# Two transformer blocks on one core: dense ones in TensorE's waits, the root spread by row tiles, weight splits moved into the last expert chunk, and two sums moved

## What is computed

```python
# first block
h = rms_norm(x, norm1_g) * (1 + sc1) + sh1
conv_out = conv_module(...)      # 31 taps, layer_norm, silu, @ w_conv_out
x = x + g1 * (mixed @ w_out)
h2 = rms_norm(x, norm2_g) * (1 + sc2) + sh2
x = x + g2 * moe_ffn(h2, ...)    # top 4 of 32
x = rms_norm(x, final_g)
# second block
x = layer_norm_2(x, ln_emb_g, ln_emb_b)
for layer in range(2):
    mix = hybrid_mixer(x, ...)   # head_group_norm of both retention directions inside
    x = layer_norm_2(ALPHA * x + mix, ln1_g, ln1_b)
    ffn = swiglu(x) if layer == 0 else moe_swiglu(x)     # top 2 of 8
    x = layer_norm_2(ALPHA * x + ffn, ln2_g, ln2_b)
```

## Time and profile before

| | |
|---|---|
| median of 3 runs | 2365.82 us (2364.69 to 2372.74) |
| profiled execution, its own time | 2366.55 us |
| span of the profiled execution | 2364.8 us |
| PE busy (matmul) | 2252.2 us, 95% of the span |
| DVE, ACT, POOL busy | 719.8, 620.7, 395.9 us |
| HBM read | 686.53 MB, mean 291 GB/s |
| mean granted clock of TensorE | 0.975 |

### The profile page before, as it was taken

How to read it: one execution, slowest core, us unless ns; L and a number is a source line. 1 busy time by engine, 2 the same in 40 slices (tenths; PEclk the granted TensorE clock), 3 DMA queues, 4 the chain that set the end, 5 groups by cost and what they waited for, 6 DMA issues and landing times.

```text
span 2364.8 us, 36121 instructions
## 1 busy us (share of the span) xinstructions
PE 2252.2 (95%) x13778; PEld 1384.6 (59%) x13779; DVE 719.8 (30%) x1376; ACT 620.7 (26%) x901; POOL 395.9 (17%) x371
## 2 busy tenths in 40 slices
PE   7999899999999999999998999999999989999898
PEld 5887744444444444444446998899998863333333
DVE  4864322222222222222226244212215341111013
ACT  2142111111111111111115671443368011111111
POOL 2000000000000000000004751688586000000000
PEclk9999799999999999999998999999999989999998
DMA  9972399999999999989994533555454375999752
GB/s 359 380 251 107 90 391 418 418 418 418 418 418 418 418 417 418 418 336 407 418 418 140 161 108 107 168 189 179 126 178 126 138 273 229 390 404 392 278 232 79
DMA packets 223487, 688.71 MB, mean 291 GB/s; under 512 B 28330, under 2 KB 117362, under 8 KB 187570
## 3 DMA queue, kind: packets, MB, share of 16 engines
q1 hardware_dynamic: 221776, 685.82, 75.7%
q10 hardware_dynamic: 1490, 1.61, 0.2%
q0 software_dynamic: 144, 0.20, 0.0%
HBM read 686.53 MB, written 1.05 MB: 291 GB/s over the span
## 4 chain that ended last, share of the span: by engine, by line
PE 66%; DMA 14%; SPq 11%; DVE 6%; issue 2%; ACT 1%; POOL 0%; ACTq 0%; DVEq 0%; POOLq 0%
PE PS L1071 16%; DMA RAW<-in_w_exp_in 10%; PE PS L698 9%; SPq L465 7%; PE PS L687 6%; PE PS L672 6%; PE PS L1173 6%; PE PS L1035 4%; PE PS L1184 3%; SPq L487 3%; DMA W<-in_w_ada 3%; PE PS L1373 3%; PE PS L1054 2%; DMA W<-in_moe_w 2%; PE PS L742 1%
## 5 line engine op out<-in xcount | busy, mean ns | idle before, releaser
L1071 PE MATMUL PS<-RAW,Z 128*64 128x512 f32 x3168 | 715.0, 598 | 23.7 <-DMA RAW<-in_w_exp_in 23.6
L407 POOL TENSOR_TENSOR WLO_D<-W,WHI_D 128x512 fp32r<-128x512 f32 x284 | 361.9, 1309 | 1174.8 <-ACT WHI_D L403 1133.2
L1071 PEld LDWEIGHTS PS<-RAW,Z 128*64 128x64 f32 x3168 | 214.0, 137 | 456.0 <-issue 376.8
L1173 PE MATMUL PS<-W,Z 128*64 128x512 f32 (+1 forms) x1056 | 212.7, 558 | 11.7 <-DMA W<-in_moe_w 11.0
L698 PE MATMUL PS<-Z,W 128*128 128x256 f32 x768 | 173.9, 388 | 5.9 <-DVE Z L2382 4.3
L403 ACT ACTIVATE WHI_D<-W 128x2048 fp32r<-128x2048 f32 x71 | 135.3, 1908 | 118.0 <-DMA W<-in_ffn_w 46.3
L698 PEld LDWEIGHTS PS<-Z,W 128*128 128x128 f32 x768 | 148.4, 194 | 28.9 <-issue 5.1
L1173 PEld LDWEIGHTS PS<-W,Z 128*64 128x64 f32 x1056 | 74.5, 137 | 150.1 <-issue 129.7
L1035 PE MATMUL PS<-Z 128*128 128x64 f32 x1088 | 128.6, 278 | 0.0
L1035 PEld LDWEIGHTS PS<-Z 128*128 128x128 f32 x1088 | 127.4, 196 | 0.4 <-issue 0.4
L2145 DVE TENSOR_TENSOR Z<-Z,PS 128x1024 f32<-128x1024 f32 x66 | 80.4, 1218 | 126.0 <-PE PS L1054 126.0
(11 more groups left out here) (400 smaller groups left out, 2704.3 us busy)
## 6 DMA issues: line engine op xcount, KB each, us to landing
RAW<-in_w_exp_in SPq DMA_DIRECT2D x256, 1024.0 KB, 19.3
RAW<-in_w_exp_out SPq DMA_DIRECT2D x128, 1024.0 KB, 21.8
W<-in_moe_w SPq DMA_DIRECT2D x128, 704.0 KB, 15.9
W<-in_w_in SPq DMA_DIRECT2D x52, 1024.0 KB, 5.8
W<-in_moe_w SPq DMA_DIRECT2D x40, 1024.0 KB, 15.7
W<-in_ffn_w SPq DMA_DIRECT2D x33, 1024.0 KB, 5.3
W<-in_w_ada SPq DMA_DIRECT2D x24, 1024.0 KB, 14.6
W<-in_w_out SPq DMA_DIRECT2D x12, 1024.0 KB, 5.0
```

The source lines that it names most:

```text
L407: i = eng.tensor_tensor(lo[:, c:c + 512], raw[:, c:c + 512], hi[:, c:c + 512].bitcast(F32), ALU.subtract)
L1071: mm = pe.matmul(ps(bank, 512, 64 * h, 64 * h + 64), x, w[:, c:c + 512], start=first, stop=final, skip_group_check=True)
L1173: mm = pe.matmul(o if b < 2 else o.rearrange("p (i n) -> p i n", i=2), X1[:, s, :], rhs, start=(s == 0), stop=(s == 7), skip_group_check=True)
```

## The change

Seven things are edited.

1. **Fillers.** `busy(n, b)` issues n matmuls of 128x512 with the constant ones as both operands into a PSUM bank that is not in use; they wait for nothing and signal nothing. They stand at: before and after the root spread of the first block's second norm (1 and 1), before the table's turn in both routings (2 and 2), after the last scatter of `experts1` (2), after the shift sum there (2) and of the last norm (2), and after the root spread of each `moments` norm (1 each).
2. **Root spread by row tiles.** `spread_root` spreads the inverse root with four matmuls that each use 32 rows and their own row tile, into four banks (`ROOTS`), in five of the six folded norms; the last norm keeps `spread`. DVE reads the operands in groups of 64 (`by_groups`).
3. **`first_jobs`** goes through pairs of k in the outer loop and the two slots inside.
4. **Head roots.** Their spread moves from behind both halves of the second `wo_attn` slot to between them, in both mixers; DVE's product with the gates of the last half moves behind the head products.
5. **Last chunk.** ACT's two high copies move from behind the token copy to behind the turn; POOL's two low parts wait for a semaphore that ACT gives after the sixth product and after the hidden layer.
6. **Convolution.** The signal for the mean is given before DVE waits for the last head's softmax.
7. `SPARE` grows to 4 columns, for ACT's signals.

```diff
-            return i if b1 == 2 else 6 + i
+            return i if b1 == 2 else 6
+
+        ROOTS = PS[:, 2:6, 0:FOLD]
...
                 for q in range(q0, q0 + 11):
+                    if q in (0, 1):
+                        pool.wait_ge(sem("m1_split_room"), q + 1)
...
-                for s in range(2):
-                    q = split_ready(lin, s)
-                    job = lin.job0 + s
-                    bank_free(job)
-                    for k in range(KT):
+                for k0 in range(0, KT, 2):
+                    for s in range(2):
+                        q = split_ready(lin, s)
+                        job = lin.job0 + s
+                        if k0 == 0:
+                            bank_free(job)
+                        for k in (k0, k0 + 1):
...
+            def spread_root():
+                stats[0] += 1
+                pe.wait_ge(sem("stat_ready"), stats[0])
+                for g in range(4):
+                    r = slice(32 * g, 32 * g + 32)
+                    mm = pe.matmul(ROOTS[:, g, :], IDENT[r, 32 * g:32 * g + 1].broadcast_to([32, P]), ROOTF[r, :],
+                                   start=True, stop=True, tile_position=(32 * g, 0), skip_group_check=True)
+                mm.then_inc(sem("stat_spread"), 1)
+
+            def busy(n, b=1):
+                for _ in range(n):
+                    pe.matmul(ps(b).rearrange("p (a n) -> p a n", a=4), ONES[:, :],
+                              ONES[:, :].unsqueeze(1).broadcast_to([P, 4, P]), start=True, stop=True)
...
                 if last:
                     spread(spread_bank(b1, 0), MEANF)
-                    spread(spread_bank(b1, 1), ROOTF)
+                    if b1 == 2:
+                        spread(spread_bank(b1, 1), ROOTF)
+                    else:
+                        spread_root()
+                    busy(1, 2 if b1 == 2 else 1)
...
                 if s == 3:
-                    spread(spread_bank(4, 1), ROOTF)
+                    busy(1)
+                    spread_root()
+                    busy(1)
...
                     tr.then_inc(sem("gates_turned"), 1)
+                busy(2, 2)
                 pe.wait_ge(sem("route_table_cols"), m.nth)
...
                 scatter_last("m1")
+                busy(2)
                 pe.wait_ge(sem("xw_ready"), 1)
                 shift_sum(XW[:, 0:2, :], 1)
+                busy(2, 2)
...
                 shift_sum(X, 3)
+                busy(2, 0)
...
-                for part in range(2):
-                    feature_job(lin, 1, z(QA, QA + 4), 4, part)
+                feature_job(lin, 1, z(QA, QA + 4), 4, 0)
...
                         if i:
                             mm.then_inc(sem("norm_sum"), 1)
+                feature_job(lin, 1, z(QA, QA + 4), 4, 1)
...
+                def room(q):
+                    act.activation(SPARE[:, q + 1:q + 2], ONES[:, 0:1], ACT.Copy).then_inc(sem("m1_split_room"), 1)
+
                 def chunk(g, split=None):
                     turned(g)
+                    if split:
+                        act.wait_ge(sem("m1_group_done"), g * 12 + 2)
+                        split()
+                        act.wait_ge(sem("m1_group_done"), g * 12 + 6)
+                        room(0)
...
                     if split:
-                        split()
+                        act.wait_ge(sem("m1_hm"), g + 1)
+                        room(1)
...
-                return bc(ps(spread_bank(b1, i), T), n)
+                if i == 0 or b1 == 2:
+                    return bc(ps(spread_bank(b1, i), T).rearrange("p (g c) -> p g c", g=4), n)
+                return bc(ROOTS, n)
...
                     taps(2)
+                    if i == 7:
+                        dve.wait_ge(sem("tap"), 4 * TAPS)
+                        dve.tensor_copy(GS[:, 16:17], GS[:, 0:1]).then_inc(sem("norm_in"), 1)
                     dve.wait_ge(sem("exp_done"), h + 1)
...
-                gated(lin, G2A, (2, 3))
+                gated(lin, G2A, (2,))
...
+                gated(lin, G2A, (3,))
                 lin = lins[f"wo_ret{l}"]
```

More of the change, by code:

```diff
@@ L309, in bc @@
         def bc(ap, n):
-            return ap.unsqueeze(1).broadcast_to([P, n, ap.shape[1]])
+            return ap.unsqueeze(1).broadcast_to([P, n] + list(ap.shape[1:]))
         def bl(ap, n):
@@ L1466, in root_table @@
             def root_table():
-                act.activation(SPARE[:, :], ONES[:, 0:1], ACT.Sqrt)
+                act.activation(SPARE[:, 0:1], ONES[:, 0:1], ACT.Sqrt)
             def norm_root(i=0):
@@ L1567, in tokens_first @@
                         .then_inc(sem("route_ht"), 1)
-                act.activation(SPARE[:, :], ONES[:, 0:1], ACT.Exp)
+                act.activation(SPARE[:, 0:1], ONES[:, 0:1], ACT.Exp)
                 act.wait_ge(sem("route_top"), m.nth)
```

27 lines of the change are left out of this document (13 added, 14 removed).

## The result

| | before | after |
|---|---|---|
| median | 2366.46 us (2364.69 to 2372.74, 4 runs) | 2341.07 us (2340.47 to 2344.17, 4 runs) |
| profiled execution, its span | 2366.55 us, 2364.8 us | 2340.47 us, 2338.7 us |
| mean granted clock | 0.975 | 0.987 |
| time at 1.2 GHz from the convolution's sums (195 us) on | about 99 us | about 42 us |

The ratio is 0.9895, with a 95% interval from 0.988 to 0.991: 25.4 us, or 1.05%, faster. The sum of the parts was 27.9 us; the spans differ by 26.1 us.

The account below looks back on a forecast made before the run. TensorE, busy 95% of the span, was taken to bound the kernel, with its waits and half-clock stretches. Eight parts sum to -27.9 us: 2366.55 to 2338.7, median 2338 us; range 2329 to 2353.

Parts of the forecast that it names:

- Convolution, -2.1: Convolution's mean: PE's sum starts at 195.9 instead of 198.67, dense work at 203.0; -2.1 us (ends -2.5 and 0).
- Second norm and routing, -6.0: First routing: faster root spread, warmer logits, clock back during the gather behind the fillers; -6.0 us (ends -9.5 and -1.5).
- Last chunk, -7.7: Last chunk and embedding norm: additions free of POOL, warm sums, statistics 1.4 us sooner; -7.7 us (-4.7 cold, -8.5 best).
- Head roots, -7.8: Both mixers' ends: earlier spread removes PE's wait for DVE and the clock loss; 2 x 3.9 us (ends -4.4 and -8).
- Norm of the first mixer and `ffn1`, -3.3: Root spread -0.5, low part bound by DVE, stage ends 1509.9 instead of 1513.1; -3.3 us (ends -0.7 and -3.5).
- `qa1`, +0.5: Feed-forward's norm: PE waits for POOL's split, clock may fall in longer idle; +0.5 us (ends -0.9 and +2.5).
- Second routing, -0.5: Second mixer's norm and routing: cold fillers end after the table, +0.8, gather about -1.6; -0.5 us (ends -1.5, +1.5).
- Last norm, -1.0: Last norm: both spreads warm, 2.2 instead of 3.68 us, fillers fit DVE's wait; -1.0 us (ends -1.8 and +0.3).
- Its signs of being wrong: Clock still falls at 269 and 1498 with fillers; a filler ends DVE's table wait; or L1850 and L1853 take longer.
- A: Fillers do not hold the clock; only moves and spreads gain, -14.4 us, so 2351 us; chance 0.20.
- B: Later waits, such as POOL's splits, DVE's contended XLO or late head products, catch gains: -11, 2355 us; chance 0.12.
- C: DVE's centring and scaling slow down reading the root from four banks: 2378 us; chance 0.06 with like mishaps.

Follow-up runs that it names:

- the hold's trace: Changed kernel with SyncE holding the 4 MB of loads behind the last chunk until the last moments' mean is there; 2335.34 us, 0.9872.
- the shift: Changed kernel with 32 small products more at the very start, moving TensorE's instruction stream by half a 16 KB piece; 2337.54 us, 0.9878.
- the run with the head's part alone: Kernel before with only the second part of the last head's job moved behind the heads' mean squares, in both mixers; 2360.43 us, 0.9972.

## Why the prediction was right, point by point

1. *Convolution, -2.1.* The first sum moved by 3.0 us (taken: 2.8). Kept was 0.54, since the clock fell at 201.1 and the second sum took 3.41 us (1.99 before). With the clock held (the hold's trace) 1.7 us more are kept, 2.2 in all. The step's end of 0, "if the longer quiet stretch costs some clock", was the case, but by chance of the execution and not by the edit.
2. *Second norm and routing, -6.0.* Measured -6.9. The logits lost the clock in their middle, as taken. It was back at 279.6, before the gather and not in it, and the fillers kept it there, which made the gather 3.3 and the first product records 1.5 us shorter. So the step "a clock that comes back during the gather" was too careful, and it did not take the fillers' dense work to bring the clock back: without them it rose at 279.3. A new idle of 0.83 us ahead of L1102 took some of it.
3. *Last chunk, -7.7.* Measured -3.6. The additions (3.26 us; taken: 3.3) and the shift sum came as computed. **The step that failed is "the last statistics come 1.4 us sooner"**: PE stopped for 3.23 us between them, waiting for its own instructions, and the clock fell at 1266.1, behind the stop. It did not fall there in the versions with fillers whose stop was short or gone. With the stop removed by the shift, the stretch from the shift sum to the second job takes 24.72 us instead of 28.54, and the part comes to -7.4.
4. *Head roots, -7.8.* Measured -4.0 and -4.0, alone -3.99 and -3.91.
5. *Norm of the first mixer and `ffn1`, -3.3.* Measured -2.35, with the clock low from 1481.1 to 1484.5; the same code in the shifted version needs 0.8 us less from the shift sum on, so the weak side is partly this execution's.
6. *`qa1`, +0.5.* Measured +0.8. PE's wait for POOL's split grew from 1.91 to 3.54 us and the clock fell at 1699.6, both as described.
7. *Second routing, -0.5.* Measured -2.2: the step "the fillers, surely cold, end after the table" failed. The clock rose at 1907.8, 0.8 us after their start, so they took 2.25 us and the gather behind them 1.95 (3.29 before).
8. *Last norm, -1.0.* Measured -1.35.

The spread was mis-sized a little everywhere: 0.45 us at full clock, not 0.6, so 0.65 saved each time (behind the last chunk, at half clock, it took 0.71). The two loops gave 1.65 us that no part had. The sum came within 2 us of the spans because parts 2, 7 and the loops gave 4.3 us more than taken, and parts 1, 3 and 5 gave 6.6 less: the mechanisms held in most parts, but the closeness of the sum is luck. Two sums of the prediction are loose: its good ends add up to 36.2 us, not 35, and its weak ends to 7.0 us, which would be 2359 and not the "weak side" of 2346; the latter was a judgement and no sum.

*Its signs of being wrong.* One of the three came true: with the fillers in place the clock still fell at 269.4 and, for 1498, at 1481.1. The forecast survived it because the stretches at half speed were shorter, 10.2 and 3.4 us instead of 27.3 and 6.8. The other two did not: in both routings the fillers end within 0.2 us of the table's last instruction, and L1850 and L1853 (now L1899, L1902) take 0.68 and 0.69 us for 512 columns as before.

*Rivals.* A put the fillers at nothing and the rest at 14.4 us: without fillers the kernel is 13.9 us faster than before, so A's sum was nearly right, and its premise, that the fillers give nothing, wrong. B named later waits; the one that caught 3 us was none of its list. C falls, DVE's operations kept their times.

*The rules cited.* That transposes do not count for the clock ("TensorE: Matmul & The Clock Gate", Part 4, of the Trainium skill) these traces leave open. Against it: in the run without fillers the clock rose at 279.3, and PE's work since the logits was four turns from 275.32, five small sums and four turns from 277.70; in the run with the head's part alone it rose at 282.9 after the same work. For it: in the kernel before, with and without the hold, the same work brought no rise. The rule on DVE and GpSimd ("SBUF — State Buffer", Who interferes with whom, of the Trainium skill) agrees: the additions, with two SBUF inputs, took 8.44 us beside GpSimd's subtractions and 3.26 us without.

## What to carry to other kernels

Dense work put into a wait is worth it where something slow and long follows the wait: two fillers, 2.46 us together in a wait, gave a gather of 3.8 us in place of 7.1. Look for it with the clock by stretch, not with the waits. And when a stretch becomes faster, look at what was never late before: here TensorE outran its own instruction stream, and 32 useless matmuls at the start, where it waited anyway, gave back the 3.8 us that this cost from the shift sum to the head sums, as much as the whole third part had brought. How far to shift is found by trying: it depends on where the borders lie.

## What the runs showed of the hardware

- TensorE's instructions come in packets of 16 KB: in straight code one for every 125 matmul records with their weight loads in the mean (76 to 166 between two of them), and none while the expert loop runs (306 to 1262 us). The Trainium skill, "Runtime: NRT & Kernel Launch", Instruction fetch mechanics, says as much: a FIFO refilled in 16 KiB blocks of 256 instructions, the next one fetched through a DMA queue of the sequencer's own while the current one runs. It calls the cost of crossing from one to the next mostly hidden; here it was 3.23 us once, and the measurement decides.
- Here the next piece was asked for about one piece ahead. In all eight traces with a stop PE went on 2.3 to 2.7 us after the packet. Counted from the record one piece ahead, the packet came after 1.2 us or less with the DMA idle or the weights at their end (eight traces, in one of them 0.2 us before that record), and after 3.0 to 3.7 us in the midst of the 4 MB of weights (six traces). The moments, 128 records of 64 columns in 2.9 us, outrun it even with the DMA idle (0.77 us of stop).
- That the piece is asked for one piece ahead is in no view; it is inferred from the places of the stops and the packets. Not settled is the 0.83 us of "issue" ahead of the first expert product (L1102). It is there in the shifted version too, so it is no such border.
